# Mixer of a hybrid decoder trunk: probabilities normalised before they meet the values, values held as the stationary operand, one output projection in three parts

## What is computed

```python
proj = h @ w_in                                 # q, k, v, z, x/B/C, dt
q, k = rms_norm(q), rms_norm(k)                 # 8 query heads, 2 key/value heads of 64
s = where(mask, q k^T * dh ** -0.5, -inf)       # window of 128: this block and the one before
m = maximum(max(s), sink)
p = exp(s - m)
denom = sum(p) + exp(sink - m)
probs = p / denom
y_attn = probs @ v
a_cum = cumsum(dt * a_coef)
decay = exp(where(tril, a_cum[l] - a_cum[s], -inf))
y_diag = (C B^T * decay) @ (x * dt)             # 8 state space heads of 64
y_ssm = rms_norm((y_diag + C h_in * exp(a_cum) + d_skip * x) * silu(z))
out = x + concatenate([y_attn, y_ssm]) @ w_out
```

## Time and profile before

| what | value |
|---|---|
| median of 3 runs | 2194.0 us |
| lowest, highest | 2193.0, 2200.44 us |
| the profiled execution | 2193.45 us, its span 2191.6 us |
| PE busy | 1959.5 us, 89% of the span |
| DVE busy | 905.1 us, 41% |
| ACT, POOL busy | 439.4, 443.4 us, 20% each |
| mixer's last matmul (L768) begins its row | 532.52 us |
| first instruction of the expert layer on PE (L1200) | 550.25 us |

### The profile page before, as it was taken

One profiled execution on the slowest core, in us unless ns is written; L12 is line 12 of the kernel. 1 busy time (PEld: TensorE's weight loads), 2 busy tenths in 40 slices (PEclk: granted clock), 3 DMA queues, 4 the chain that ended last, 5 costly groups with the idle time before them and its releaser, 6 DMA issues. The chain is left out here.

```text
span 2191.6 us, 47668 instructions
## 1 busy us (share of the span) xinstructions
PE 1959.5 (89%) x20910; PEld 1196.8 (55%) x20910; DVE 905.1 (41%) x1917; ACT 439.4 (20%) x982; POOL 443.4 (20%) x555
## 2 busy tenths in 40 slices
PE   6999999997599988889969999998969989889992
PEld 4766667774456545555545444444656655545561
DVE  2555565453631111111137999994262111111114
ACT  2333322221511100111124212232321101001110
POOL 2211110110222322222222111110102222222220
PEclk9999999999799999999989999999859999999996
DMA  9000000000889999999958552410369999999986
GB/s 330 2 1 1 1 1 0 0 1 1 327 373 404 424 424 424 404 420 426 421 193 232 111 112 69 96 34 10 142 237 392 417 429 422 419 421 403 425 362 239
DMA packets 102938, 523.25 MB, mean 239 GB/s; under 512 B 23462, under 2 KB 57306, under 8 KB 86352
## 3 DMA queue, kind: packets, MB, share of 16 engines
q1 hardware_dynamic: 74328, 463.00, 51.7%
q0 software_dynamic: 25504, 48.83, 8.0%
q10 hardware_dynamic: 2904, 8.44, 1.0%
HBM read 496.56 MB, written 34.65 MB: 242 GB/s over the span
## 5 line engine op out<-in xcount | busy, mean ns | idle before, releaser
L1259 PE MATMUL ps<-wgu,xT 128*32 128x256 f32 x10752 | 632.4, 389 | 2.6 <-DVE xT L1407 2.6
L1259 PEld LDWEIGHTS ps<-wgu,xT 128*32 128x32 f32 x10752 | 345.5, 112 | 252.4 <-issue 33.1
L1414 DVE TENSOR_TENSOR hh<-sg,ps 128x128 f32<-128x128 f32 x168 | 66.5, 396 | 653.8 <-ACT sg L1087 653.4
L1274 PE MATMUL ps<-wd,hhT 128*32 128x256 f32 x5376 | 320.2, 379 | 0.0
L1148 POOL DMA_INDIRECT y_rows<-my,yidx x168 | 166.8, 993 | 749.0 <-ACT my L1081 727.7
L1885 DVE SCALAR_TENSOR_TENSOR acc<-u,par,acc 128x512 f32<-128x512 f32 x381 | 255.8, 744 | 0.0
L1274 PEld LDWEIGHTS ps<-wd,hhT 128*32 128x32 f32 x5376 | 172.3, 110 | 117.8
L1087 ACT ACTIVATE sg<-ps 128x128 f32<-128x128 f32 x168 | 46.6, 277 | 715.8 <-PE ps L1259 715.8
L709 PE MATMUL ps<-w_in_sb,hn 128*128 128x512 f32 (+1 forms) x384 | 147.9, 540 | 6.0 <-DVE hn L536 6.0
L1241 PE MATMUL ps<-ident,xg 128*128 128x128 f32 x512 | 77.3, 299 | 68.0 <-DMA xg<-h_rows,hidx 67.9
L1407 DVE TENSOR_TENSOR xT<-ps,g_exp 128x384 f32<-128x384 f32 (+2 forms) x128 | 59.0, 502 | 174.2 <-PE ps L1241 174.2
(11 more groups left out here) (311 smaller groups left out, 1807.1 us busy)
## 6 DMA issues: line engine op xcount, KB each, us to landing
wgu<-in_moe_w_gate_up SPq DMA_DIRECT2D x64, 4096.0 KB, 19.7
wd<-in_moe_w_down SPq DMA_DIRECT2D x64, 2048.0 KB, 18.7
conv<-prod POOLq DMA_DIRECT2D x42, 256.0 KB, 3.2
w_in_sb<-in_w_in SPq DMA_DIRECT2D x4, 2048.0 KB, 14.5
h_rows<-wgu ACTq DMA_DIRECT2D x16, 512.0 KB, 6.3
wg<-in_conv_w_pw SPq DMA_DIRECT2D x16, 512.0 KB, 4.3
wa<-in_conv_w_pw SPq DMA_DIRECT2D x16, 512.0 KB, 5.7
wgu<-y_rows SPq DMA_DIRECT2D x16, 512.0 KB, 10.2
```

The lines of the kernel that those rows point to most:

```text
L1259: mm = pe.matmul(ps[TB * g:TB * g + TB, GU + n % 2, 0:2 * P].rearrange("p (a f) -> p a f", a=2), xT[:, q % 2, j, TB * tl:TB * tl + TB], wg ...
L1274: mm = pe.matmul(ps[TB * g:TB * g + TB, Y + n % 2, 0:D // 4], hhT[:, n % 2, TB * j:TB * j + TB], wd[:, q % 3, j, D // 4 * g:D // 4 * g + D ...
```

## The change

The probabilities are divided by their denominator in s, before they are turned (normalise_probs on DVE, once for each key head), and turn_probs waits for that. ACT takes exp(sinkm) for each key head right behind its probabilities. L839's matmul has its operands exchanged: the values, 64 columns, are stationary, and the probabilities of four heads, 512 columns, move; the two key heads write the two halves of the partitions of one PSUM bank. The product is then attention already turned, so turn_y has four transposes instead of eight, and DVE copies the product straight into attn_T, which is half of yT for even chunks and half of ycat for odd ones. w_out's upper half is loaded in two transfers by key head to fit the new order of rows, so w_out comes in three. The cumulated decay of a head is spread over rows by a transpose of one column of acum, repeated 128 times, and ua is gone from POOL. In the last turn project_out(6) is in three parts: its first half of columns where it was, four matmuls of the second half between the two turn_probs, the other four behind the state products; project_out(7) writes other banks (B6, B7), and yT_evacuate(7) comes before add_to_x(6).

```diff
...
@@ -237,2 +236,3 @@
         rows = ycat[0:ROWS, :]
+        attn_T = (yT[:, 0:4, :], ycat[:, 0:DI].rearrange("p (k t) -> p k t", k=4))
...
@@ -265,3 +266,3 @@
         PJ0, PJ1, TR, S4, S5, B6, B7 = 0, 1, 2, 4, 5, 6, 7
-        out_banks = lambda c: (PJ1, PJ0) if isinstance(c, int) and c == NT - 2 else (PJ1, B7)
+        out_banks = lambda c: {NT - 2: (PJ1, PJ0), NT - 1: (B6, B7)}.get(c, (PJ1, B7)) if isinstance(c, int) else (PJ1, B7)
@@ -291,3 +292,5 @@
             sp.dma_start(x[:, 1:NT, :], tiles[:, 1:NT, :]).then_inc(x_loaded, 16)
-            sp.dma_start(w_out[:, :, :], I["w_out"].rearrange("a (k p) n -> p (a k) n", p=P)).then_inc(wo_loaded, 16)
+            for g in range(NKV):
+                sp.dma_start(w_out[DH * g:DH * g + DH, 0:4, :], I["w_out"][0, 4 * DH * g:4 * DH * g + 4 * DH, :].rearrange("(k p) n -> p k n", p=DH)).then_inc(wo_loaded, 16)
+            sp.dma_start(w_out[:, 4:8, :], I["w_out"][0, DI:D, :].rearrange("(k p) n -> p k n", p=P)).then_inc(wo_loaded, 16)
             load_router(k, sp, 0)
@@ -352,5 +355,3 @@
                 pool.wait_ge(dt_ready, c + 1)
-                link(pool.tensor_tensor(a[:], dt[:, p, :], a_coef[:], ALU.mult))
-                pool.tensor_tensor(ua[:], upper[:, :].unsqueeze(1).to_broadcast([P, NS, P]),
-                                   a[:, :].unsqueeze(2).to_broadcast([P, NS, P]), ALU.mult).then_inc(ua_ready, 1)
+                pool.tensor_tensor(a[:], dt[:, p, :], a_coef[:], ALU.mult).then_inc(a_ready, 1)
...
@@ -491,2 +492,3 @@
                                    accum_out=den[:, g, j:j + 1]).then_inc(probs_ready, 1)
+                act.activation(esink[:, g, :], sinkm[:, g, :], ACT.Exp).then_inc(esink_ready, 1)
@@ -508,6 +510,5 @@
                 act.wait_ge(seg_ready, c + 1)
-                act.activation(se[:], sm[:], ACT.Exp).then_inc(esink_ready, 1)
+                act.activation(se[:], sm[:], ACT.Exp).then_inc(se_ready, 1)
                 act.activation(dec[:], seg[:], ACT.Exp).then_inc(dec_ready, 1)
                 probs(c, 1)
-                act.activation(esink[:], sinkm[:], ACT.Exp).then_inc(esink_ready, 1)
                 if nxt:
...
@@ -605,2 +606,9 @@

+            def normalise_probs(c, g):
+                dve.wait_ge(probs_ready, 8 * c + 4 * g + 4)
+                dve.wait_ge(esink_ready, 2 * c + g + 1)
+                link(dve.tensor_tensor(den[:, g, :], den[:, g, :], esink[:, g, :], ALU.add))
+                link(dve.reciprocal(rden[:, g, :], den[:, g, :]))
+                dve.tensor_tensor(s[:, g, :, :], s[:, g, :, :], rden[:, g, :].unsqueeze(2).to_broadcast([P, 4, 2 * P]), ALU.mult).then_inc(normed, 1)
+
             def yT_evacuate(c):
@@ -609,3 +617,2 @@
                     dve.wait_ge(o_done, 2 * c)
-                dve.tensor_copy(yT[:, 0:4, :], ps[:, TR, :].rearrange("p (k t) -> p k t", k=4)).then_inc(yT_ready, 1)
                 dve.tensor_tensor(yT[:, 4:8, :], ps[:, TR + 1, :].rearrange("p (k t) -> p k t", k=4),
@@ -657,4 +664,7 @@
                 scores(c, p, 1)
+                normalise_probs(c, 0)
                 if nxt:
                     qk_norm(c + 1)
+                normalise_probs(c, 1)
+                if nxt:
                     convolve(c + 1, 1 - p, 0)
@@ -662,11 +672,6 @@
                 dve.wait_ge(pv_done, c + 1)
-                dve.wait_ge(esink_ready, 2 * c + 2)
-                dve.wait_ge(probs_ready, 8 * c + 8)
-                link(dve.tensor_tensor(den[:], den[:], esink[:], ALU.add))
-                link(dve.reciprocal(rden[:], den[:]))
-                for g in range(2):
-                    heads = lambda ap: ap.rearrange("p (j b d) -> p b j d", b=2, d=DH)
-                    dve.tensor_tensor(heads(ycat[:, 256 * g:256 * g + 256]), heads(ps[:, S4, 256 * g:256 * g + 256]),
-                                      rden[:, g, :].rearrange("p (b j) -> p b j", b=2).unsqueeze(3).to_broadcast([P, 2, 2, DH]),
-                                      ALU.mult).then_inc(pv_out, 1)
+                if not (isinstance(c, int) and c < 2):
+                    dve.wait_ge(o_done, 2 * c - 2)
+                dve.tensor_copy(attn_T[p].rearrange("p (j b) t -> p b j t", b=2), ps[:, S4, :].rearrange("p (b j t) -> p b j t", b=2, j=2)).then_inc(pv_out, 1)
+                dve.wait_ge(se_ready, c + 1)
@@ -694,4 +699,4 @@
             turns(dve, turn)
-            add_to_x(NT - 2)
             yT_evacuate(NT - 1)
+            add_to_x(NT - 2)
             add_to_x(NT - 1)
@@ -749,3 +754,3 @@
             def turn_probs(c, g):
-                pe.wait_ge(probs_ready, 8 * c + 4 * g + 4)
+                pe.wait_ge(normed, 2 * c + g + 1)
                 for slot in range(2):
@@ -757,4 +762,3 @@
                 pe.wait_ge(ycat_ready, c + 1)
-                pe.wait_ge(pv_out, 2 * c + 2)
-                for j in range(KD):
+                for j in range(4, KD):
                     mm = pe.transpose(ps[:, TR + j // 4, (j % 4) * P:(j % 4 + 1) * P], ycat[:, j * P:(j + 1) * P], ident[:])
@@ -762,11 +766,17 @@

-            def project_out(c, nxt=None):
-                pe.wait_ge(wo_loaded, 16)
-                pe.wait_ge(yT_ready, 2 * c + 2)
-                for half, bank in enumerate(out_banks(c)):
-                    for j in range(KD):
-                        mm = pe.matmul(ps[:, bank, :], yT[:, j, :], w_out[:, j, 512 * half:512 * half + 512], start=(j == 0), stop=(j == KD - 1))
+            def project_part(c, p, half, j0, j1):
+                bank = out_banks(c)[half]
+                for j in range(j0, j1):
+                    mm = pe.matmul(ps[:, bank, :], attn_T[p][:, j, :] if j < 4 else yT[:, j, :], w_out[:, j, 512 * half:512 * half + 512], start=(j == 0), stop=(j == KD - 1))
+                if j1 == KD:
                     mm.then_inc(o_done, 1)
-                    if half == 0 and nxt is not None:
-                        turn_hn(*nxt)
+
+            def project_out(c, p, nxt=None):
+                pe.wait_ge(wo_loaded, 16 * 3)
+                pe.wait_ge(pv_out, c + 1)
+                pe.wait_ge(yT_ready, c + 1)
+                project_part(c, p, 0, 0, KD)
+                if nxt is not None:
+                    turn_hn(*nxt)
+                project_part(c, p, 1, 0, KD)
@@ -778,3 +788,3 @@
                 if not first:
-                    pe.wait_ge(pv_out, 2 * c)
+                    pe.wait_ge(pv_out, c)
                     pe.wait_ge(y_out, c)
@@ -794,3 +804,3 @@
                 pe.wait_ge(sx_ready, c + 1)
-                pe.wait_ge(ua_ready, c + 1)
+                pe.wait_ge(a_ready, c + 1)
                 for g in range(2):
@@ -801,3 +811,3 @@
                 if not first:
-                    pe.wait_ge(yT_ready, 2 * c)
+                    pe.wait_ge(yT_ready, c)
                 for t in range(6):
@@ -813,4 +823,5 @@
                 pe.wait_ge(cb_out, c + 1)
-                pe.matmul(ps[:, B7, :], ones[:], ua[:, 0:4, :].rearrange("p h l -> p (h l)"), start=True, stop=True)
-                pe.matmul(ps[:, B6, :], ones[:], ua[:, 4:8, :].rearrange("p h l -> p (h l)"), start=True, stop=True).then_inc(rows_done, 1)
+                for h in range(NS):
+                    mm = pe.transpose(ps[:, B7 if h < 4 else B6, (h % 4) * P:(h % 4 + 1) * P], acum[:, h:h + 1].to_broadcast([P, P]), ident[:])
+                mm.then_inc(rows_done, 1)
                 pe.wait_ge(s_out, 2 * c + 1)
@@ -821,5 +832,10 @@
                 if not nxt:
-                    project_out(c - 1)
+                    pe.wait_ge(wo_loaded, 16 * 3)
+                    pe.wait_ge(pv_out, c)
+                    pe.wait_ge(yT_ready, c)
+                    project_part(c - 1, 1 - p, 0, 0, KD)
                 pe.wait_ge(xb_out, 2 * c + 2)
                 turn_probs(c, 0)
+                if not nxt:
+                    project_part(c - 1, 1 - p, 1, 0, 4)
                 if nxt:
@@ -835,6 +851,5 @@
                 pe.wait_ge(pT_ready, 4 * c + 4)
-                for h in range(NH):
-                    g, j = h // 4, (h % 2) * 2 + h % 4 // 2
-                    for slot in range(2):
-                        mm = pe.matmul(ps[:, S4, h * DH:(h + 1) * DH], pT[:, g, slot, j, :], v[:, slot, g * DH:(g + 1) * DH],
+                for slot in range(2):
+                    for g in range(NKV):
+                        mm = pe.matmul(ps[DH * g:DH * g + DH, S4, :], v[:, slot, g * DH:(g + 1) * DH], pT[:, g, slot, :, :].rearrange("p j q -> p (j q)"),
                                        start=(slot == 0), stop=(slot == 1))
@@ -848,2 +863,4 @@
                 mm.then_inc(y_done, 1)
+                if not nxt:
+                    project_part(c - 1, 1 - p, 1, 4, KD)
                 if nxt:
@@ -855,3 +872,3 @@
                         pe.wait_ge(y_out, c + 1)
-                        project_out(c - 1, (c + 2, p) if nxt2 else None)
+                        project_out(c - 1, 1 - p, (c + 2, p) if nxt2 else None)
                 elif nxt2:
@@ -861,4 +878,4 @@
             turn_y(NT - 1)
```

(4 more changed lines are left out.)

10 lines of the change are left out of this document (5 added, 5 removed).

## The result

The changed kernel takes 2165.27 us (median of four executions, 2156.77 to 2172.22), the kernel before 2193.69 (four, 2193.0 to 2200.44). The ratio is 0.9879, with a 95% interval of 0.9848 to 0.9909: 26.5 us faster by the ratio, 28.4 by the medians. Forecast were 18.6, and the result lies 0.7 us under the lower end of the range. The profiled execution took 2166.62 us, with a span of 2164.9, so 26.8 us under that of before.

The account below looks back on a forecast made before the run. TensorE's own work was taken to bound the mixer. Turns 1 to 6 save 9.9 us, turn 0 1.4, the last turn 7.3: 18.6 off 2193.45 gives 2175 us, range 2166 to 2184.

Parts of the forecast that it names:

- rival (a): Middle turns: TensorE does not wait for normalised probabilities; about 9 us more saved over seven turns, 2166 us; chance 0.10.
- L854: Probabilities times values: two column halves run at once, 1.9 us for 3.57, saving 1.67 a turn; bounds 1.72 and 3.6.
- rival (b): Probabilities times values: the halves run one behind the other, 3.44 us, losing 13 us in eight turns, 2188; chance 0.06.
- Rows of decay: Cumulated decay spread by eight transposes: 0.87 us for 1.81, saving 0.94 a turn, a repeated column loading like others.
- The wait of normalise_probs: Before a middle turn's first turn_probs: TensorE waits 1.3 us for DVE, leaving net 0.1 of 1.38 saved there.
- I move POOL by 1.1: Middle turn: POOL's products come 1.1 us earlier, the rows' 1.3 less some 0.2 for ACT's extra small exponential.
- Turns 0 to 2: First turns of the mixer: 1.4 us saved in turn 0, 1.65 in each of turns 1 and 2.
- The last turn: Mixer's last turn: its output projection starts at 525.2 instead of 532.52, saving 7.3 us.
- Rival (c): Last turn: wait for scores(1) grows from 2.24 to over 3 us and lowers the clock, costing 1.9 to 3; 2178; chance 0.14.
- Hidden work: Second normalise_probs, 1.8 us of cover, and the 0.7 us attention copy delay TensorE by nothing in a middle turn.
- Slower (d): Every turn's 1.3 us wait lowers the clock, costing 15 to 28 us over eight turns; 2194 to 2203; chance 0.05.
- moves all that follows by as much: Behind the mixer: experts' first weights are asked for after its end, so an earlier end shifts everything later equally.

Follow-up runs that it names:

- pv_same_half: Changed kernel with both key heads' values multiplied into partitions 0 to 63, head by head, so half the attention is wrong; 2167.40 us (one execution).
- norm_first: Changed kernel with VectorE's normalise_probs(c, 0) ahead of scores(c, p, 1) instead of behind it; median 2157.65 us of five executions, ratio to before 0.9858.
- after_third: The changed kernel itself, unedited, traced a third time; mixer's end at 532.5 us, 1625.6 us behind the mixer.
- pv_by_group: Changed kernel with the four matmuls of probabilities times values issued key head by key head instead of in turn; 2170.23 us (one execution).
- later_20: Changed kernel with 184 idle transposes ahead of its last output projection, so the mixer ends at 550.6; 2182.78 us (twelve executions), ratio to before 0.997.
- out_whole: Changed kernel with project_out(6) in one piece ahead of both turnings of the probabilities, instead of three; 2165.69 us (one execution).

## Why the prediction came out as it did

The mechanism of each term of the sum held; the mixer was forecast 18.6 us shorter and is 19.8 (17.7 to 21.1 with the repeats). The median came lower than the forecast by 9.7 us. In the profiled execution it is 8.3, of which 1.2 lie in the mixer and 7.0 behind it, where the forecast had nothing. By the time alone (2165.27) rival (a), with its 2166, would have been taken for right; the trace shows that it was not.

**L854.** 1.9 us forecast, 1.87 measured. The experts' columns were the right rows, and pv_same_half shows that it is the two halves at once. Its bound of 3.6 is what the same half costs, 3.58. The Trainium skill (TensorE: Matmul & The Clock Gate, section "The mechanism") lets a weight load overlap matmuls only when the row group differs; here the row groups are the same, and 1.88 against 3.58 disagrees with the use that rival (b) made of it. The same page's section "Measured speedup vs the span model" gives 2.38 for three tiles of 32 columns, which goes the way of the trace: 3.58 / 1.88 is 1.9 for two of 64. The rival fell. What I left out is the change of mode for the neighbours: L848 went from 1.74 to 1.82 and L859 from 0.92 to 0.97, start to start, 0.13 a turn together.

**Rows of decay.** 0.94 forecast, 0.85 measured: 0.96 for eight transposes, not 0.87. The next instruction is the scores in halves of the rows, and going over to them costs 0.09; so it did before, when L814 took 0.86 and L815 0.95. My 1.81 had that in it and my 0.87 had not. That a repeated column loads as fast as others held. **turn_y**: 0.44, as forecast.

**The wait of normalise_probs.** Right in kind, wrong in size: 1.3 forecast from start to start, 1.07 measured (258.42 is where TensorE's queue would have come to the turning, 259.49 where it started; the bracket says 0.91, since the end of a length has some 0.16 in it). The step that failed is "I move POOL by 1.1": a small exponential more on ACT, I held, would take 0.2 of the shift. GpSimd moved by all that TensorE did. Before, ACT stood idle for 0.83 us, waiting for DVE, ahead of L509 (at 259.79), which is next to the exponential that GpSimd's products wait for (L510), and the small one found room there. So GpSimd's second product came 7.00 us after the start of the rows before (255.26 to 262.26) and 6.15 after (249.42 to 255.57), 0.85 less, which is all that the rows gave. The sum's hold, the 0.3 and the 1.22 came within 0.1 of what was worked out. Sum of the turn: 1.57 + 0.85 + 0.44 - 1.07 = 1.79, measured 1.74, forecast 1.65. Rival (a) fell with the bracket of 0.91, and norm_first put its price at 1.1 a turn. Here the Trainium skill (SBUF — State Buffer, section "SBUF: two separate sides") tells of an exclusive lock that holds the loser entirely. The trace agrees: 1.01 for 0.16. In norm_first GpSimd's 1.49 for 1.27 goes the same way, though the product ends some 0.14 us sooner than a hold up to the multiply's end (252.55) would have it.

**Turns 0 to 2.** 1.4 + 2 x 1.65 = 4.7 forecast, 5.42 measured. The surplus is clock, and chance: turn 1's first projection stands behind a wait of 4.24 us in both, and took 9.59 us before, 8.62 after, but 9.95 in after_third.

**The last turn.** 7.3 forecast, 7.14 measured, but by another way. From the turn's start:

| place | forecast | measured |
|---|---|---|
| second scores | 8.7 | 8.67 |
| first turning of the probabilities | 18.05 | 18.41 |
| second turning | 22.4 | 22.71 |
| transposes of ycat | 35.5 | 35.93 |
| last projection | 37.3 | 37.46 |

Rival (c), to which I gave 0.14, came: wait 3.08, clock 0.54, 1.9 us over the 6.9 that the sixteen records were costed at. Its price is nearly nothing here, which I had not seen: the wait of 1.4 that the forecast put right behind them was its cover, and 0.36 is what was left. Two traces where the clock stayed at 1.00 show it, pv_by_group and later_20: the cover is there again as a wait of 1.11 and 1.12 us, the first turning comes 18.00 after the turn's start, as forecast, and the transposes of ycat 35.55, 0.38 earlier than in the table. What the low clock takes shows only once the cover is gone: in norm_first the first turning comes 19.54 after the turn's start, and more in out_whole. That the longer wait brought the clock down is right in eight traces of eleven; what decides between them stays open. The clock in the last projection cost 1.7 us (5.32 for 3.60), against 1.9 before, so the 2 that I left out cancels in the difference.

**Hidden work** stayed hidden: the second turning has no wait (267.53), and in turns 0 to 2 TensorE has no idle time beyond those of before, but for the new one ahead of the first turning.

**Slower (d)** fell: the clock is 1.00 through the middle turns, with 0.91 to 1.04 us of idle time in each turn from 0 to 6.

**Behind the mixer**, "moves all that follows by as much" held where it could be tested (later_20: 18.1 us of mixer, 17.2 of time). The step that failed is what the sum stands on, that nothing else differs between two executions. The same code there took 1625.6 to 1634.4 us in three traces of the changed kernel, whose times lie up to 21 us apart within one set (2157.70 to 2178.46), and before's profiled execution, from which the sum was made, was one with the second router at 37.3 us and not 22.0. The forecast's range had no term for that.
